# Attention on one core: the extra tokens' product moved from first to last in the output sum

## The reference

```python
s_band = einsum('bnqkgd,bnskd->bnkgqs', qb, k_band) * scale     # window of 128 keys
s_meta = einsum('bnqkgd,bmkd->bnkgqm', qb, k_meta) * scale      # the 16 extra tokens
probs  = softmax(concatenate([sink, s_meta, s_band]))
p_meta, p_band = probs[..., 1:17], probs[..., 17:]
o = einsum('bnkgqm,bmkd->bnqkgd', p_meta, v_meta) + einsum('bnkgqs,bnskd->bnqkgd', p_band, v_band)
return o @ w_o + b_o
```

## Time and profile before

| what | value |
|---|---|
| median of 3 runs | 2126.72 us (2124.92 to 2140.71) |
| the profiled execution's own time | 2125.48 us |
| its span, first to last instruction | 2123.4 us |
| PE, PEld busy | 91%, 75% of the span |
| DVE, ACT, POOL busy | 74%, 59%, 18% |
| mean granted clock of the matrix engine | 0.959 of full |
| the attention phase | about 1209 to 1440 us |

### The profile page before, as it was taken

How to read it: one execution, slowest core, us unless ns; L and a number is a source line. 1 busy time by engine, 2 the same in 40 slices (tenths; PEclk the granted TensorE clock), 3 DMA queues, 4 the chain that set the end, 5 groups by cost and what they waited for, 6 DMA issues and landing times. The chain is left out here.

```text
span 2123.4 us, 31683 instructions
## 1 busy us (share of the span) xinstructions
PE 1933.1 (91%) x10634; PEld 1586.2 (75%) x10634; DVE 1579.3 (74%) x1767; ACT 1249.6 (59%) x1532; POOL 375.3 (18%) x674
## 2 busy tenths in 40 slices
PE   4949999959999999999699999996899999999991
PEld 3648777748888888888598777775788888888880
DVE  8996321368999999999752286656699999999995
ACT  6614210427777777777540165544477777777771
POOL 2000000302222222221233100002122222222214
PEclk9979999979999999999799999998899999999995
DMA  4174300439999999999712010006499999999986
GB/s 104 24 76 154 99 1 1 179 131 363 388 384 380 379 379 380 384 387 391 256 60 71 29 63 1 2 1 261 158 366 367 381 383 388 393 394 394 391 317 248
DMA packets 136172, 504.69 MB, mean 238 GB/s; under 512 B 38610, under 2 KB 68626, under 8 KB 84882
## 3 DMA queue, kind: packets, MB, share of 16 engines
q1 hardware_dynamic: 114786, 468.72, 59.7%
q0 software_dynamic: 18432, 33.86, 4.2%
q10 hardware_dynamic: 2880, 1.12, 0.4%
HBM read 488.47 MB, written 47.32 MB: 252 GB/s over the span
## 5 line engine op out<-in xcount | busy, mean ns | idle before, releaser
L1734 DVE TENSOR_TENSOR moe_lo<-moe_raw,moe_hi 128x2048 fp32r<-128x2048 f32 x378 | 860.8, 2291 | 91.5 <-ACT moe_hi L1509 76.7
L1509 ACT CAST moe_hi<-moe_raw 128x2048 fp32r<-128x2048 f32 x374 | 711.9, 1916 | 131.2 <-PE moe_ps_g L1899 56.2
L1897 PE MATMUL moe_ps_g<-moe_hi,moe_x_hi 128*128 128x512 f32 x512 | 207.6, 405 | 5.0 <-DVE moe_lo L1734 3.0
L1897 PE MATMUL moe_ps_y<-moe_hi,moe_h_hi 128*128 128x512 f32 x512 | 205.6, 402 | 3.8 <-DVE moe_h_lo L1750 3.8
L1899 PE MATMUL moe_ps_g<-moe_lo,moe_x_hi 128*128 128x512 f32 x512 | 201.2, 393 | 0.0
L1898 PE MATMUL moe_ps_g<-moe_hi,moe_x_lo 128*128 128x512 f32 x512 | 201.1, 393 | 0.0
L1899 PE MATMUL moe_ps_y<-moe_lo,moe_h_hi 128*128 128x512 f32 x512 | 200.7, 392 | 0.0
L1898 PE MATMUL moe_ps_y<-moe_hi,moe_h_lo 128*128 128x512 f32 x512 | 200.5, 392 | 0.0
L1899 PE MATMUL moe_ps_u<-moe_lo,moe_x_hi 128*128 128x512 f32 x512 | 199.7, 390 | 0.0
L1897 PE MATMUL moe_ps_u<-moe_hi,moe_x_hi 128*128 128x512 f32 x512 | 199.2, 389 | 0.0
L1898 PE MATMUL moe_ps_u<-moe_hi,moe_x_lo 128*128 128x512 f32 x512 | 199.2, 389 | 0.0
(11 more groups left out here) (482 smaller groups left out, 3717.7 us busy)
## 6 DMA issues: line engine op xcount, KB each, us to landing
moe_raw<-moe_w_gate SPq DMA_DIRECT2D x128, 1024.0 KB, 7.6
moe_raw<-moe_w_up SPq DMA_DIRECT2D x128, 1024.0 KB, 8.7
moe_raw<-moe_w_down SPq DMA_DIRECT2D x128, 1024.0 KB, 9.3
mix_r<-ssm_w_glu SPq DMA_DIRECT2D x16, 512.0 KB, 5.3
xn_dram<-moe_work SPq DMA_DIRECT2D x16, 512.0 KB, 8.2
prj_yc<-y_dram SPq DMA_DIRECT2D x8, 1024.0 KB, 6.9
moe_raw<-y_dram SPq DMA_DIRECT2D x8, 1024.0 KB, 12.0
mix_r<-x SPq DMA_DIRECT2D x8, 512.0 KB, 5.1
```

Source lines behind the costliest of these rows:

```text
L1509: A.copy(hi[:, slot(number, k), :], raw[:, k, :]).then_inc(hi_done, 1)
L1734: V.tensor_tensor(lo[:, slot, :], raw[:, k, :], hi[:, slot, :].bitcast(F32), ALU.subtract).then_inc(lo_done, 1)
L1897: T.matmul(out, x_h, w_h, start=first, stop=False)
```

## The change

In `outputs`, the extra tokens' product is issued last in place of first. The window products now clear the sum (`start=True`), and the extra tokens' product ends it and raises `pv_mm`. Number, operands and shapes of all products stay; so do the waits, which stay in the same order among themselves. The extra tokens' product now stands directly ahead of `transpose_weights`, and the window products directly behind `scores`.

```diff
                 outs = [ps_o[r * DH:(r + 1) * DH, 0:P] for r in range(H2)]
-                T.matmul(ps_o[:, 0:P], v_meta[:, c // 2, :], pt[0:3 * N_META, s % 2, 2 * P:], start=True, stop=False)
                 for r in range(H2):
-                    last = T.matmul(outs[r], v_sb[:, max(i - 1, 0), vc], pt[:, s % 2, r * P:(r + 1) * P], start=False, stop=(i == 0))
+                    T.matmul(outs[r], v_sb[:, max(i - 1, 0), vc], pt[:, s % 2, r * P:(r + 1) * P], start=True, stop=False)
                 if i:
                     pe.wait_ge(own_set, s - DC + 1)
                     pe.wait_ge(v_step_set, i)
                     for r in range(H2):
-                        last = T.matmul(outs[r], v_step[:, i % 2, vc], p_own[:, s % 2, r * P:(r + 1) * P], start=False, stop=True)
-                last.then_inc(pv_mm, 1)
+                        T.matmul(outs[r], v_step[:, i % 2, vc], p_own[:, s % 2, r * P:(r + 1) * P], start=False, stop=False)
+                T.matmul(ps_o[:, 0:P], v_meta[:, c // 2, :], pt[0:3 * N_META, s % 2, 2 * P:], start=False, stop=True).then_inc(pv_mm, 1)
```

## The result

The changed kernel takes 2137.88 us (median of 8 runs, 2136.67 to 2146.75) against 2125.82 for the kernel before (8 runs, 2122.11 to 2140.71). The ratio is 1.0054, 95% interval 1.0029 to 1.0079: slower by about 12 us, clear of the scatter, and inside the 1% in which the prediction put it.

The account below looks back on a forecast made before the run. PE's chain of products and pauses was taken to bound the attention. 61 steps at 0.195 us gave 11.9 us on 2125.48, so 2137.4, or 2138.6 on the median; forecast 2138 us, range 2130 to 2145.

Parts of the forecast that it names:

- The rival by which the new pauses would fall into PE's wait for `o_lo`: Ahead of `outputs`: longer pauses are taken back at the next step, up to 0.195 us each; 2126 us, chance 3%.
- Which forms are one form: In the array, 48 rows count with the scores' 64 rows and not with 128; only changes between forms cost.
- transposes count with the extra tokens' product: Rival: going from 48 rows to full size costs nothing, 0.34 against 0.30 us a step; 2128 us, chance 6%.
- Scores to window products: First form change in the new step: 0.09 pause plus 0.05 load, 0.14 us; bounds 0 and 0.20.
- Correction to extra tokens' product: Form change from 128*64 to 48*128 in the new step: 0.19 to 0.20 us; bounds 0.14 and 0.25.
- Extra tokens' product to transposes: Last form change in the new step: 0.10 pause plus 0.06 load, 0.16 us; bounds 0 and 0.20.
- The count: Of 64 runs of `outputs`, the 61 with scores ahead pay 0.195 us each, 11.9 us; three behind the projection don't.
- The way to the end: After the attention's last addition: the delay reaches the end in full, since nothing of the next phase runs ahead.
- The clock: Rival: the clock falls in the attention, 19 us of it at the 1.2 GHz level; about 2150 us, chance 4%.
- ACT's new wait for the transposes: ACT's copy directly behind the transposes in each step will wait for them, about 0.15 to 0.2 us.
- The margin ahead of the correction: `p_own` is ready 1.19 us before the next step's correction; with the wait for `own_set` moved up, 0.9 remains.
- idle by issue in four places of the step, not three: Sign in the changed profile: idle time that no engine ended stands ahead of operand loads at four places per step.

Follow-up runs that it names:

- the run with the full-size form last: Changed kernel with the extra tokens' operands zero-padded from 48 to 128 contraction rows; 2126.61 us, ratio 1.0003 to the kernel before.
- the first version in twos: Kernel before with its steps taken in twos, the output sum given two banks and the transposes one; 2130.32 us, ratio 1.0031.
- the second: Kernel before with steps in twos, products grouped by form, sums read a step later, projections' additions ahead of `o_lo`; 2116.92 us, ratio 0.9956.

## Why the prediction was right

- The bound. PE was taken as a chain of products and pauses with no wait in it. The changed loop grew by 12.0 us against 11.9 forecast. The run with the waits moved showed that the margins were real. The rival by which the new pauses would fall into PE's wait for `o_lo` did not come either: `o_lo` is ready 0.70 ahead of the load that waits for it, and every steady step grew by the full 0.20.
- Which forms are one form. The reading that 48 rows go with 64 and not with 128 rested on the earlier trace rows. The two padded runs settled it: padding turned the change into no loss, and turned the kernel before into one of the change's size. The rival "transposes count with the extra tokens' product" fell: the changed kernel's 0.42 from that product to the transposes is 0.22 of streaming, 0.10 of load and 0.10 of pause.
- The prices that no row of before showed. Scores to window products: 0.09 + 0.05 forecast; measured 0.66 - 0.57 = 0.09 ahead of it and 324 ns in place of 272. Correction to extra tokens' product: 0.19 to 0.20 forecast; measured 0.32 - 0.22 = 0.10 and 0.10 of load (373 ns and not 271). Extra tokens' product to transposes: 0.16 forecast, 0.10 and 330 ns in place of 272 measured. The step of 3.53 is the forecast to the hundredth. The last price came from the mixer's row, the other two from neighbours of another kind, so part of this closeness is luck.
- The count. 61 steps at 0.195. The three sums behind the projection cost nothing extra. The last of them lies between the last transposes and the last addition, where both kernels need 15.8 us. The two before it end up 0.16 us shorter together, and that is a wait for `o_lo` that went: it was 0.24 at 1419.18 in the kernel before.
- The way to the end. All 12 us arrived there.
- The clock. From 1243 to 1428 us the changed kernel was granted 1.00, and its mean over the run is 0.960 against 0.959, so the rival by which it would fall didn't come.

Three small things were off, and the sum hung on none of them. ACT's new wait for the transposes was put at 0.15 to 0.2 us and is 0.29:

```profile
1328.31 0.37 ACT L2100 COPY att_pt<-att_ps_t 128x256 f32<-128x256 f32 x1 [0.29 <-PE att_ps_t L2232]
```

The margin ahead of the correction was to shrink from 1.19 to 0.9 and is still 1.17. And "idle by issue in four places of the step, not three" was misjudged: the view has two such places before and three after, since a load that the trace shows still running covers the pause behind it, as ahead of the transposes now. The distance of starts on PE showed every seam, the idle times did not.

The pauses themselves, loads left out, measured 0.09 to 0.10 in the change too. The Trainium skill's figure for the way out of the array ("TensorE: Matmul & The Clock Gate", section Drain, about 128 cycles, an estimated 0.053 us at 2.4 GHz) would have given about 2135, an estimate again; the page gives it for the end of a single product and not for a change of mode, and the measured pauses decide. The rule of the Trainium skill ("TensorEngine Tiling (Array Packing)", section Key Properties) that a change of tiling mode drains the engine fits the pauses of 0.09 to 0.10 us that stand at every change between 64 and 128 contraction rows, and between 64 and 128 output rows, in the steps read here. That such a pause is a drain no run here shows.

What stays open is what the 0.09 to 0.10 consists of; no run separated the end of the last product from the start of the next load. Open too is how output rows are counted: the transposed strip, 128\*48, stands between full-size products without a pause (in the run with the full-size form last, 0.21 us from L2230 to L2233 where two products stream 0.22, then 0.35 from L2233 to L2264 where streaming is 0.11 + 0.23), while the correction with 64 output rows pays 0.10 ahead of the transposes.

## What to carry to other kernels

Where small products of different forms share the matrix engine, count the seams between forms in a step and price each as a pause plus the first load of the new form, from the distance of starts in the timeline; what counts is the rows that the product takes in the array, not the columns that it streams. In these runs 48 contraction rows counted with 64 and not with 128, and the products with 64 output rows not with those of 128. Put a short product beside neighbours of its own form, or pad it to theirs. Fewer seams pay only as long as the other engines' chain still fits under the products: the first version in twos lost more to waits than it saved, the second read the sums a step later and kept its saving. Don't add the waits of the load queue and of the product queue; they can be the same wait.

## What the runs showed of the hardware that was not expected

Padding a product from 48 to 128 contraction rows costs next to nothing by itself: in the run with the full-size form last, its two instructions take 0.11 us of streaming each as before, and the shorter of them lasts 275 ns where the unpadded one has 272. What padding changes is which neighbours cost a pause. And a product's exposed load of 128 columns costs the same 0.10 us whether it has 48 rows (373 against 272 ns in the changed kernel) or 128 (378 against 275 ns):

```profile
L2251 PE MATMUL att_ps_o<-att_pt,att_v_meta x128: 275/326/378, 1217.2 to 1431.1; 128*128 128x128 f32 x128
```
